# Spreading the gates by two rounded products instead of one plain product

## What is computed

```python
idx  = jnp.take_along_axis(cand_i, top_pos, axis=-1)   # 128 of 16384 experts a token
gate = jax.nn.softmax(top_s, axis=-1)
act  = jax.nn.gelu(jnp.einsum('td,ted->te', xb, jnp.take(u, ib, axis=0)))
out  = jnp.einsum('te,ted->td', gb * act, jnp.take(v, ib, axis=0))
```

## Time and profile before

| | |
|---|---|
| timed runs | 3580.07, 3580.40, 3585.87 us |
| span of the profiled execution, first to last instruction | 3575.0 us |
| TensorE products, busy | 3398.0 us (95%) |
| TensorE weight loads, busy | 3333.7 us (93%) |
| VectorE | 2760.2 us (77%) |
| ScalarE | 1201.3 us (34%) |
| GpSimd | 2199.5 us (62%) |

### The profile page before, as it was taken

How to read it: one execution, slowest core, us unless ns; L and a number is a source line. 1 busy time by engine, 2 the same in 40 slices (tenths; PEclk the granted TensorE clock), 3 DMA queues, 4 the chain that set the end, 5 groups by cost and what they waited for, 6 DMA issues and landing times.

```text
span 3575.0 us, 58964 instructions
## 1 busy us (share of the span) xinstructions
PE 3398.0 (95%) x22379; PEld 3333.7 (93%) x22379; DVE 2760.2 (77%) x4360; ACT 1201.3 (34%) x1885; POOL 2199.5 (62%) x1426
## 2 busy tenths in 40 slices
PE   7899989989999989999999999999999999999997
PEld 6899979988999979999999999999999999999975
DVE  5515467667887666999989899753898989998877
ACT  3310131232221232465665656542222222222242
POOL 5578865323678655666666666665666666666544
PEclk9999989999999999999999999999999999999998
DMA  4233432111688768889888988997888899988812
GB/s 152 79 117 123 136 108 79 56 49 65 215 311 313 279 217 290 281 307 326 310 324 303 335 304 323 322 354 258 314 309 312 310 312 314 315 311 311 282 60 94
DMA packets 326530, 856.15 MB, mean 239 GB/s; under 512 B 27856, under 2 KB 125648, under 8 KB 323024
## 3 DMA queue, kind: packets, MB, share of 16 engines
q0 software_dynamic: 110592, 402.70, 31.3%
q1 hardware_dynamic: 74592, 260.24, 21.5%
q10 hardware_dynamic: 141168, 190.87, 15.4%
HBM read 758.82 MB, written 94.90 MB: 239 GB/s over the span
## 4 chain that ended last, share of the span: by engine, by line
PE 71%; DVE 14%; issue 4%; DMA 3%; POOL 3%; ACT 3%; ACTq 1%; SPq 0%; DVEq 0%; POOLq 0%
PE main L720 52%; PE main L965 12%; PE scr L918 4%; DMA raw<-stream 3%; DVE scr L1729 2%; POOL v_lo L675 2%; POOL rows L626 1%; DVE rows L1722 1%; ACTq L1350 1%; DVE h L2104 1%; PE scr L818 1%; PE scr L735 1%; ACT v_hi L1360 1%; DVE res L2210 1%; DVE h_lo L2109 1%
## 5 line engine op out<-in xcount | busy, mean ns | idle before, releaser
L592 POOL TENSOR_TENSOR w_lo<-raw,w_hi 128x1024 fp32r<-128x1024 f32 x206 | 529.0, 2568 | 403.6 <-ACT w_hi L1064 397.7
L720 PE MATMUL main<-mix_hi,w_hi 128*128 128x320 f32 (+1 forms) x2816 | 684.7, 317 | 29.6 <-DVE mix_lo L1552 9.9
L720 PE MATMUL main<-mix_lo,w_hi 128*128 128x320 f32 (+1 forms) x2816 | 672.7, 313 | 0.0
L720 PE MATMUL main<-mix_hi,w_lo 128*128 128x320 f32 (+1 forms) x2816 | 672.6, 313 | 0.0
L626 POOL DMA_INDIRECT rows<-v_rows,s_idx x384 | 388.9, 1013 | 365.1 <-DVE scr L1729 290.9
L1729 DVE SCALAR_TENSOR_TENSOR scr<-rows,s_dot,scr 128x1024 f32<-128x1024 f32 x381 | 487.5, 1279 | 49.5 <-DMA rows<-v_rows,s_idx 31.5
L965 PE MATMUL main<-h_hi,v_hi 128*128 128x320 f32 x2048 | 473.2, 312 | 39.3 <-DVE res L2115 36.3
L720 PEld LDWEIGHTS main<-mix_hi,w_hi 128*128 128x128 f32 x2816 | 476.3, 189 | 34.0 <-issue 19.6
L720 PE MATMUL main<-a_hi,w_hi 128*128 128x320 f32 (+1 forms) x1728 | 466.7, 324 | 24.8 <-DVE a_lo L1552 8.8
L626 POOL DMA_INDIRECT rows<-u_rows,s_idx x384 | 399.0, 1039 | 137.0 <-issue 69.4
L720 PEld LDWEIGHTS main<-mix_lo,w_hi 128*128 128x128 f32 x2816 | 480.0, 189 | 0.0
(11 more groups left out here) (273 smaller groups left out, 5283.4 us busy)
## 6 DMA issues: line engine op xcount, KB each, us to landing
raw<-stream SPq DMA_DIRECT2D x478, 512.0 KB
act_d<-actb ACTq DMA_DIRECT2D x128, 320.0 KB
gate_d<-gbuf ACTq DMA_DIRECT2D x20, 2048.0 KB, 9.4
h<-act_d ACTq DMA_DIRECT2D x128, 320.0 KB
gate_in<-gate_d ACTq DMA_DIRECT2D x31, 1280.0 KB
rows<-u_rows,s_idx POOLq DMA_INDIRECT x384
rows<-v_rows,s_idx POOLq DMA_INDIRECT x384
score_d<-stage ACTq DMA_DIRECT2D x16, 320.0 KB
```

What stands on the lines that cost most here:

```text
L592: pool.tensor_tensor(w_lo[:, s, :], raw[:, s, :], w_hi[:, s, :].bitcast(F32), ALU.subtract) \
L720: last = pe.matmul(main[s][:, dst:dst + n], wt[:, s, c * P:(c + 1) * P], rows[:, c, src:src + n], start=(c == 0 and wt is w_hi and rows is ...
```

## The change

The product of one-hots and weighted one-hots is made in the rounded format. A gate in 32 bits doesn't fit that format, so it is split in a rounded part and the rest, and the token's table becomes the sum of two products, accumulated in PSUM: key 2's one-hot times key 1's one-hot weighted with the rounded part, and the same times that weighted with the rest. unpack gains two VectorE instructions per block, on 128 x 128 elements, which make the two parts (gate_part). weigh_hots gains one ScalarE instruction per token, which writes the one-hot weighted with the rest into a new tensor hot_low (two halves of 4 tokens); the old instruction then weighs in place with the rounded part. hot and oh take the rounded type; qrow's first alias is a tensor of its own at the same place. No wait and no semaphore is added or taken away.

```diff
-        hot = nc.alloc_sbuf_tensor_at("hot", [P, DC, T], F32, offset=res0)
+        hot = nc.alloc_sbuf_tensor_at("hot", [P, DC, T], F32R, offset=res0)
+        qrow0 = nc.alloc_sbuf_tensor_at("qrow0", [P, DC, T], F32, offset=res0)[:, 0:2, 0:TS]
...
-        qrow, keys = [hot[:, 0:2, 0:TS], qrow1], [keys0, keys1]
+        qrow, keys = [qrow0, qrow1], [keys0, keys1]
...
-        oh = nc.alloc_sbuf_tensor_at("oh", [P, DC, P], F32, offset=set2 + 40 * 1024)
+        gate_part = [lay(f"gate_part{i}", [P, 2, P], F32R) for i in range(2)]
+        hot_low = nc.alloc_sbuf_tensor_at("hot_low", [P, 2, 4, NKEYS], F32R, offset=set2 + 44 * 1024)
+        oh = nc.alloc_sbuf_tensor_at("oh", [P, DC, P], F32R, offset=set2 + 40 * 1024)
...
                     for k in range(4):
-                        last = pe.matmul(scr[1][:, w * HALF + k * P:w * HALF + (k + 1) * P],
-                                         hot_key(half + w, 1, k), hot_key(half + w, 0, k), start=True, stop=True)
+                        dst, key = scr[1][:, w * HALF + k * P:w * HALF + (k + 1) * P], hot_key(half + w, 1, k)
+                        pe.matmul(dst, key, hot_key(half + w, 0, k), start=True, stop=False)
+                        last = pe.matmul(dst, key, hot_low[:, w, k, :], start=False, stop=True)
                     last.then_inc(gates_filled, 1)
...
                         key = hot_key(2 * m + w, 0, k)
-                        ins = act.activation(key, key, ACT.Copy, scale=packed[j % 2][:, 2, col:col + 1])
+                        act.activation(hot_low[:, w, k, :], key.bitcast(F32), ACT.Copy,
+                                       scale=gate_part[j % 2][:, 1, col:col + 1].bitcast(F32))
+                        ins = act.activation(key, key.bitcast(F32), ACT.Copy,
+                                             scale=gate_part[j % 2][:, 0, col:col + 1].bitcast(F32))
                     ins.then_inc(oh_act, 1)
...
                 dve.sem_inc(sel_drained, 1)
+                gate, part = packed[j % 2][:, 2, :], gate_part[j % 2]
+                steps.then(dve.tensor_copy(part[:, 0, :], gate))
+                steps.then(dve.tensor_tensor(part[:, 1, :], gate, part[:, 0, :].bitcast(F32), ALU.subtract))
```

## The result

The changed kernel takes 3611.9 us, the median of four runs (3609.3 to 3613.4); the kernel before 3580.35 in the same comparison. The ratio is 1.0088 with an interval of 1.0073 to 1.0102. The kernel became slower, by 31.6 us where 12.5 were forecast, and 3611.9 lies above the range that ended at 3605.

What follows compares the result with a forecast made beforehand. TensorE was taken to bound the edited stage, its own part costing 0; stalls from ScalarE's extra weighings and unpack, 8.9 + 2.0 + 0.4 + 1.2 = 12.5 us, on 3580.4 gave 3593 us, range 3581 to 3605.

Steps and rivals of the forecast that it cites:

- VectorE and GpSimd otherwise have time: Rest of the edited stage: VectorE idles 15 us of each block, so one-hots and casts cost 0.
- the full clock of TensorE: Edited stage: TensorE read as busy all 184 us of a block at 2.4 GHz; no clock loss was priced.
- TensorE's part, 0: Quarters' products: 1280 pairs stay 1280, paced by weight loads at 107 to 112 ns; 0, bounds -5 to +11 us.
- ScalarE per quarter: Sixteen weighings take 2.36 us more; a full iteration takes 8.73 of 8.82 us, so an undisturbed quarter costs 0.
- Softmax, 8.9: Quarter behind the softmax in each of four blocks: weighing ends late, TensorE stalls 2.2 us each, 8.9 in all.
- First quarter, 2.0: Stage's first quarter: two unpack instructions (0.9 us) and the longer weighing make its second half 2.0 us later.
- Turn of the sparse tokens, 0.4: Once, at the sparse tokens' turn: Gelu 1.1 us late, weights come at 9.83 against 9.41 us, 0.4 lost.
- Late Gelus, 1.2: Two places where Gelu is 1.26 us late for buffer or DMA ahead of a full iteration: 0.6 each, 1.2 us.
- One sign: Records of the quarters' products: each rounded product was to be shorter by some 50 ns.
- slower than forecast: Rival: ScalarE's 0.09 us of spare is gone or a pair takes 120 ns; +22, 3602 us; chance 0.15.
- my law of columns: Rounded products: 0.42 ns a column plus 13 ns, giving 67 ns at 128 columns; 67 ns pairs had chance 0.08.

Runs made afterwards that it cites:

- e6: Changed kernel with 64 instead of 128 moving columns in the two rounded products of a quarter (half of each table missing): 3610.6 us, one execution.
- e7: Changed kernel with 64 instead of 128 columns of key 2's one-hot loaded as weights in the rounded products (half of each table missing): 3600.4 us.
- e2: Changed kernel without the added weighing with the rest; both rounded products take the rounded part: 3582.0 us, ratio 1.0011 to the kernel before.
- e12: Kernel before with only the two new VectorE instructions in unpack, their result unused: 3580.3 us, ratio 1.0001.
- e1: Kernel before with eight more ScalarE weighings per quarter, into a tensor nobody reads; products stay plain, 128 columns: 3597.2 us, ratio 1.0051.
- e11: Changed kernel with fewer VectorE dots per expert tile in the stage and more behind it: 3645.9 us, ratio 1.0177 to the kernel before.
- e5: Changed kernel with the exponential of the four softmaxes in the stage replaced by a copy, so no table loads there: 3598.0 us, ratio 1.0038.
- e8: Changed kernel without the two VectorE instructions in unpack; both weighings use the gate as it is: 3605.3 us, ratio 1.0070 to the kernel before.
- e9: e1 with plain products of 64 instead of 128 moving columns (half of each table missing): 3603.6 us, ratio 1.0065 to the kernel before.
- e3: Changed kernel where TensorE multiplies ready operands instead of waiting at the first quarter and behind each softmax: 3606.0 us, ratio 1.0074.
- e4: Changed kernel with one rounded product and one weighing per token, the rest of the gate dropped: 3562.3 us, ratio 0.9949 to the kernel before.

## Why the prediction was wrong, step by step

Two steps failed. "VectorE and GpSimd otherwise have time" put at nothing what the trace shows as 4.1 us of waits in block four. And the full clock of TensorE was taken as given behind the new waits too, where the stage lost 9.9 us to 1.2 GHz. Term by term:

- **TensorE's part, 0: right.** 1280 pairs at 112.0 ns, paced by the load (e6, e7), and no cost in the time without the weighings (e2). The Trainium skill, TensorE: Matmul & The Clock Gate, section Back-to-back issue gap, gives 81 ns as the sustained pace of products of 128 columns; for this format the measurement, 112 with a load of 128 columns, decides.
- **ScalarE per quarter: right.** 16 weighings take 4.8 us; an undisturbed full iteration mostly 8.7 to 8.8 us of 8.82, and TensorE doesn't wait there: the 0.09 us of spare held.
- **Softmax, 8.9: right,** 9.0.
- **First quarter, 2.0: too small,** 2.9. The two instructions cost 0.6, not 0.9 (from the copy's start to the one-hot's 1.28 us, before 0.70). But the first one-hot took 3.33 us instead of 1.2: GpSimd's w_lo had begun at 1471.11, 0.29 us ahead of it, and ran until 1473.65; the one-hot ended 1.08 later. Before, the second one-hot was the slow one. So the first half of the quarter waited too, 1.85 us, which I had not looked for. The two instructions alone cost nothing to be seen (e12 has no wait there), and the weighings alone bring a wait of 1.6 us ahead of the second half (e1). The Trainium skill, SBUF — State Buffer, section SBUF: two separate sides, says that a VectorE instruction with two operands in SBUF and one of GpSimd that reads SBUF exclude each other for a whole instruction; these two rows agree.
- **Turn of the sparse tokens, 0.4: right,** 0.39. **Late Gelus, 1.2: 2.2,** three places of 0.7 and not two of 0.6.
- **Sum of these: 14.5 measured, 12.5 forecast.** The mechanism and its size were right.
- **One sign was wrong.** The rounded product's record was to be some 50 ns shorter; it is 271 to 277 ns against 275. The slopes over wide products don't show in the record of one of 128 columns, so the 53 ns of product in a pair stays an estimate.
- **"VectorE and GpSimd otherwise have time": wrong, 4.1 us.** I read VectorE's 15 us of idle time per block as cover. That was the mean over a block. In block four its one-hots come 4.02 us late, 2.9 of them because a w_lo of GpSimd stands in their way; e1 has the same wait, so the second weighing is enough for it. e11 takes the wait away by taking dots away, and with it the collision. In e5, e6, e8 and e9 it is another wait, 6.2 to 6.3 us at the fourth softmax's quarter, where VectorE is still picking the next keys and no one-hot is slow. Which small shift brings which of the two stays open.
- **No term for the clock: wrong, 9.9 us in the stage.** I wrote down that TensorE runs at its full clock through the whole block, and didn't ask what happens to it once waits are put next to products half as long. That they are half as long stood in the same paragraph, as 53 ns of product in a pair of 112 ns. e9 and e3 show the two conditions; in e5 the waits behind the softmaxes and the clock cost there fall together.
- **Behind the stage: 5.4 us, open.** In the profiles stretches at 1.2 GHz add up to 41 us there before and 52 after, and e12, whose stage is as long as before's within 2 us, has 56 us of them and 1118.6 us behind the stage. So at least a part isn't of the change; how much, a profile each can't tell.
- **The range ended at 3605** because its upper case, "slower than forecast", added 8 to 11 us for ScalarE or the pair, which both came as forecast; the 14 us from the clock and VectorE had no case.

Waits 14.5 + 4.1 + 0.8, clock 9.9, behind the stage 5.4, ahead of it -1.0: 33.7 of the 33.8 us by which the spans differ.

## What to carry to other kernels

When an edit puts waits on TensorE, price them twice: the wait, and what the clock does behind it, above all where the products around it are shorter than their weight loads: here 20 us of waits brought another 10, and in e1, with 18 us of them around longer products, 2.4. Cover must be read where it is used: 73 us of idle ScalarE a block covered every ordinary quarter with 0.09 us to spare and failed at four known places, and 15 us of idle VectorE a block did not cover one-hots that stood 2.9 us behind a w_lo. If a split into two products isn't needed for precision, one rounded product gains on both sides (e4). When you move work of one engine within a stage, ask which queue behind it (here GpSimd's fetches and w_lo) waits for the moved part.

## What the runs showed of the hardware

- A rounded product of 128 moving columns with a load of 64 columns repeats every 60 ns, below the 67 ns by my law of columns; with a load of 128 it is 112 ns, with 64 or 128 moving columns alike.
- Waits of 0.8 and 1.4 us around eight rounded pairs were followed by 1.2 GHz for 3.4 to 6.8 us at three of the four softmaxes of the changed kernel, and at all three in e8 where the wait was this short (as in e9, with plain products of 64 columns). Around plain pairs of 128 columns (e1) they were at none of four; its one stretch in the stage (at 2170.4, 6.8 us) stands behind the longer wait of block four, 2.2 us. Why the changed kernel's first softmax was spared, and what exactly decides, stays open.
- A one-hot of 1.2 us took 3.33 next to a GpSimd operation of 2.54 that began just ahead of it. This is common: before 24 of 160 one-hots take over 2 us, in the changed kernel 21, up to 4.13 us, and every one of them ends 1.08 or 1.09 us behind the end of a w_lo.
